# The low parts of four expert units go from VectorE to GpSimd, their high parts go ahead of the second norm's root on ScalarE

## What is computed

```python
        mix = jnp.concatenate([rec, att], axis=-1) @ w_out[l]
        x = x + g1[:, None, :] * mix
        h2 = _rms(x, norm2_g[l]) * (1.0 + sc2[:, None, :]) + sh2[:, None, :]
        x = x + g2[:, None, :] * _hier_moe(h2, w_rg[l], b_rg[l], w_re[l], b_re[l], w1[l], w3[l], w2[l])

def _hier_moe(h, w_rg, b_rg, w_re, b_re, w1, w3, w2):
    g_logits = hf @ w_rg + b_rg                     # best of 4 groups
    e_logits = (hf @ w_re + b_re).reshape(-1, 4, 4) # best 2 experts of that group
    ...
    for e in range(N_EXPERTS):                      # 16
        he = jax.nn.silu(hf @ w1[e]) * (hf @ w3[e])
        y = y + combine[:, e:e + 1] * (he @ w2[e])
```

## Time and profile before

| | us |
|---|---|
| runs before, median of 3 (lowest, highest) | 1921.34 (1917.24, 1923.22) |
| profiled execution, whole | 1922.14 |
| its span, first to last instruction | 1920.5 |
| TensorE busy | 1845.2 |
| VectorE busy | 1441.2 |
| ScalarE busy | 990.5 |
| GpSimd busy | 163.8 |

### The profile page before, as it was taken

How to read it: one execution, slowest core, us unless ns; L and a number is a source line. 1 busy time by engine, 2 the same in 40 slices (tenths; PEclk the granted TensorE clock), 3 DMA queues, 4 the chain that set the end, 5 groups by cost and what they waited for, 6 DMA issues and landing times.

```text
span 1920.5 us, 28821 instructions
## 1 busy us (share of the span) xinstructions
PE 1845.2 (96%) x11109; PEld 1627.7 (85%) x11109; DVE 1441.2 (75%) x1550; ACT 990.5 (52%) x953; POOL 163.8 (9%) x149
## 2 busy tenths in 40 slices
PE   7999999999999999999999999998998589999999
PEld 6888899998888788889999888877996478888886
DVE  7555786857877765577785787786687698888888
ACT  4444566534444444446563444443344357777774
POOL 1000000000000000000000000001000134323401
PEclk9999999999999999999999999998997799999999
DMA  6555455554877455544556377755340289999995
GB/s 245 197 191 183 154 202 189 203 198 150 287 253 268 164 186 197 190 163 173 193 181 241 132 271 255 253 185 174 122 135 20 75 316 368 348 366 348 365 352 197
DMA packets 61698, 417.33 MB, mean 217 GB/s; under 512 B 7344, under 2 KB 7712, under 8 KB 13728
## 3 DMA queue, kind: packets, MB, share of 16 engines
q1 hardware_dynamic: 51392, 369.19, 53.8%
q0 software_dynamic: 10192, 46.75, 7.3%
q10 hardware_dynamic: 16, 0.01, 0.0%
HBM read 405.94 MB, written 9.98 MB: 217 GB/s over the span
## 4 chain that ended last, share of the span: by engine, by line
PE 82%; DVE 10%; DVEq 3%; issue 2%; ACT 2%; ACTq 1%; DMA 0%; POOL 0%; POOLq 0%
PE ps L1751 14%; PE ps L1750 7%; PE ps L1735 7%; PE ps L1737 7%; PE ps L1736 7%; PE ps L1852 4%; PE ps L1853 4%; PE ps L1856 4%; PE ps L840 4%; PE ps L841 4%; PE ps L842 4%; PE ps L1748 2%; DVE wlo L2185 2%; PE ps L869 2%; PE ps L871 2%
## 5 line engine op out<-in xcount | busy, mean ns | idle before, releaser
L2185 DVE TENSOR_TENSOR wlo<-raw,whi 128x2048 fp32r<-128x2048 f32 x236 | 538.2, 2289 | 194.3 <-ACT whi L2017 191.6
L2017 ACT ACTIVATE whi<-raw 128x2048 fp32r<-128x2048 f32 x236 | 450.9, 1911 | 271.6 <-PE ps L1737 113.9
L1751 PE MATMUL ps<-xT,whi 128*128 128x512 f32 x1232 | 440.3, 397 | 0.0
L1750 PE MATMUL ps<-xT,wlo 128*128 128x256 f32 x1232 | 344.5, 280 | 0.1
L1751 PEld LDWEIGHTS ps<-xT,whi 128*128 128x128 f32 x1232 | 231.8, 188 | 47.7
L1735 PE MATMUL ps<-xT,whi 128*128 128x256 f32 x928 | 264.0, 285 | 2.0 <-DVE xT L2196 2.0
L1736 PE MATMUL ps<-xT,whi 128*128 128x256 f32 x928 | 263.8, 284 | 0.0
L1737 PE MATMUL ps<-xT,wlo 128*128 128x256 f32 x928 | 263.7, 284 | 0.0
L1750 PEld LDWEIGHTS ps<-xT,wlo 128*128 128x128 f32 x1232 | 233.0, 189 | 8.9 <-DVE xT L2204 1.0
L1438 DVE TENSOR_TENSOR wlo<-raw,whi 128x2048 fp32r<-128x2048 f32 x76 | 175.0, 2304 | 20.2 <-ACT whi L1060 19.4
L2041 ACT ACTIVATE rest<-ps 128x512 f32<-128x512 f32 x88 | 52.5, 597 | 250.7 <-PE ps L1751 250.7
(11 more groups left out here) (478 smaller groups left out, 3408.9 us busy)
## 6 DMA issues: line engine op xcount, KB each, us to landing
raw<-stream SPq DMA_DIRECT2D x236, 1024.0 KB, 4.9
raw<-experts SPq DMA_DIRECT2D x76, 1024.0 KB, 7.3
mod<-experts SPq DMA_DIRECT2D x38, 1024.0 KB, 6.8
adaraw<-ada POOLq DMA_DIRECT2D x24, 1024.0 KB, 5.2
yd<-lnrow POOLq DMA_DIRECT2D x17, 512.0 KB, 8.2
lnrow<-ln_g POOLq DMA_DIRECT2D x6, 512.0 KB, 5.0
lnrow<-ln_b POOLq DMA_DIRECT2D x6, 512.0 KB, 6.2
x_sb<-x SPq DMA_DIRECT2D x1, 1024.0 KB, 5.2
```

The costliest lines, as they stand in the source:

```text
L1750: nc.tensor.matmul(bank(b, T), wl, xThi[:, k, :], start=False, stop=False)
L1751: return nc.tensor.matmul(bank(b), wh, both, start=False, stop=k == KD - 1)
L2017: act_fn(whi[:, slot, :], raw[:, slot, :], ACT.Copy).then_inc(hi_done, 1)
L2185: v.tensor_tensor(wlo[:, slot, :], raw[:, slot, :], whi[:, slot, :].bitcast(F32), ALU.subtract).then_inc(lo_done, 1)
```

## The change

GpSimd gets an `expert_lo` of its own and runs it for units 0 to 3, behind the two DMAs of L592 and behind a wait for the stream's last low part. VectorE loses these four subtractions, and gets a wait that all four low parts are there. ScalarE makes the high parts of units 0 to 2 ahead of `rms_root("2")`, and that of unit 3 behind `split_xT`. The fifth and sixth buffer for raw numbers change places, and with them the wait of the load that fills the one in `mod`.

```diff
-        raws = [raw[:, 0, :], raw[:, 1, :], raw[:, 2, :], mod[:, 0:UNIT], mod[:, UNIT:2 * UNIT], raw5[:, :]]
+        raws = [raw[:, 0, :], raw[:, 1, :], raw[:, 2, :], mod[:, 0:UNIT], raw5[:, :], mod[:, UNIT:2 * UNIT]]
...
-                elif p == 4:
+                elif p == 5:
                     sp.wait_ge(x_done, 4 * N_H2 + 4)
...
+            def expert_lo(p):
+
+                if p < RING:
+                    pool.wait_ge(used, UNITS - (UNITS - 1 - p) % RING)
+                pool.wait_ge(*expert_hi_done(p))
+                g.tensor_tensor(splits[p % SPLITS][1], raws[p % RAWS], splits[p % SPLITS][0].bitcast(F32),
+                                ALU.subtract).then_inc(lo_done, 1)
...
+            pool.wait_ge(lo_done, RING + UNITS)
+            for p in range(SPLITS):
+                expert_lo(p)
             pool.wait_ge(ev["zero_row"], 32)
...
-            rms_root("2")
-            split_xT(N_H2)
...
-            expert_hi(0)
+            for p in range(RING):
+                expert_hi(p)
+            rms_root("2")
+            split_xT(N_H2)
+            expert_hi(RING)
...
-            for p in range(1, SPLITS):
-                expert_hi(p)
...
-            expert_lo(0)
             for pair in range(4):
                 select(0, pair)
                 if pair == 0:
                     first_one_hot(1)
-            for p in range(1, SPLITS):
-                expert_lo(p)
+
+            unit_split(dve, SPLITS - 1)
```

## The result

The changed kernel takes 1930.78 us (median of 9 runs, 1927.06 to 1934.54). The kernel before takes 1922.93 us beside it (9 runs, 1916.71 to 1924.34). The ratio is 1.0044, with a 95% interval of 1.0033 to 1.0056. The forecast was 1930.5 us, slower: 9.2 us on a kernel before of 1921.34, where 7.85 us on 1922.93 was measured. The profiled execution took 1930.89 us, with a span of 1929.2 us, 8.7 us more than before.

The account below looks back on a forecast made before the run. TensorE bounds the experts, and the chain through the second norm sets when they begin. Three holds of VectorE, together +9.76 us, less 0.6 for the first copy, give +9.2 on 1921.34: 1930.5 us, range 1920 to 1935.

Parts of the forecast that it names:

- What bounds the kernel: Experts are TensorE's once the first product begins at 1547.19; the second norm is on the path, each us added counts.
- ScalarE's part: Three high parts of 1.90 us each ahead of the second norm's root, where ScalarE idles 15.16 us, cost nothing.
- The first copy: VectorE's first subtraction leaves the chain before the copy of gathered tokens: gain 0.6 us, bounds 0 and 2.19.
- GpSimd's price: One GpSimd subtraction of 2048 columns takes 4.70 us, doubled from a row of 1024 columns; upper bound 6.0.
- Its start: GpSimd's first subtraction starts at 1505.87, when its queue is no longer occupied.
- What the rows of before showed of the meeting: At 1552.74 GpSimd's 256-column operation and VectorE's small one each waited for the other, taking 1.75 and 0.63 us.
- The handover: In the second norm, GpSimd's and VectorE's two-operand operations exclude each other, the waiting one first: 2.23, 2.91, 4.62, together 9.76 us.
- the bounds of the forecast: If GpSimd goes on at once, three in a row, L1417 is late by 11.6 us: 1932.3; with 6.0 us each, 1935.
- Low part 3: Its 4.70 us end at 1526.9, 0.5 before the routing's next two-operand operation, L1464 at 1527.42: costs nothing.
- Pieces: Ports shared in short pieces: some 10 VectorE operations lose 0.19 us each, 2 us at most: 1922.7; chance 0.17.
- hidden: VectorE's small operations pass GpSimd's subtractions; only the first-copy gain of 0.6 to 2.19 is left: 1920.7 to 1919.2; chance 0.11.
- one meeting: GpSimd's subtractions slide behind the norm, one at most in the way: +2.2 to +4.7, less 0.6, 1923 to 1925.4; chance 0.06.

Follow-up runs that it names:

- experiment 1: Changed kernel with the four low parts back on VectorE, ScalarE's new order and the buffers kept: 1919.86 us, ratio to the kernel before 0.9996.
- experiment 7: The changed kernel, unchanged, run again for its distribution and a second trace: 1929.53 us, ratio to the kernel before 1.0034.
- Experiment 3: Changed kernel, but GpSimd clears the four low parts (a write with no read) instead of subtracting: 1922.11 us, ratio to the kernel before 1.0001.
- Experiment 2: Changed kernel with a pipeline drain behind each of GpSimd's four subtractions: 1929.20 us, ratio to the kernel before 1.0045.
- experiment 5: Changed kernel with only the first low part on GpSimd, the other three back on VectorE behind the copies: 1920.09 us, ratio to the kernel before 0.9994.
- experiment 9: Changed kernel with 16 zero matmuls on TensorE, eight ahead of the second half's attention transposes and one behind each head's: 1930.23 us.
- experiment 11: Changed kernel with zero matmuls at the attention transposes, GpSimd copying the raw units instead of subtracting: 1921.42 us, ratio to the kernel before 1.0000.
- experiment 10: Kernel before with zero matmuls at the attention transposes, plus 40 ahead of the tokens' turning, 60 and 40 in the routing's waits: 1919.58 us, ratio 0.9993.

## Why the prediction was right, and where it was not

**What bounds the kernel: right.** The time is that of the first product plus 373.3 to 373.4 us, and the second norm is on the path to it.

**ScalarE's part at nothing: right** (experiment 1). The other edits at nothing: no wait of TensorE in the experts has come in.

**The first copy, 0.6 us: too much.** It starts 2.11 us after the gather (1550.07 on VectorE) instead of 2.39 (1541.59 - 1539.20), so 0.28 is gained. The last eight gather products then took 1.44 us instead of 1.20, and the first product stands 7.97 us behind the gather's start, where it stood 7.99: in this execution nothing of the gain arrives. In experiment 7, the same kernel, those eight took 1.21 us and the distance is 7.74 (1553.77 - 1546.03), so there 0.25 arrives, still less than half of what the forecast had.

**GpSimd's price, 4.70: near.** 4.49 to 4.55 us. The Trainium skill's 4497 ns (GPSIMD Engine Reference, Elementwise — side-by-side cycle accounting) is what the trace shows, and the doubled row of 1024 columns was 0.2 too high. **Its start, 1505.87:** it was 1504.16, as its two small DMAs were through 1.7 us sooner. What sets that was not tried.

**What the rows of before showed of the meeting: read too widely.** The operation that lasted 0.63 us beside GpSimd is a TENSOR_SCALAR with one operand, not an operation with two inputs like those that the rule quoted by the forecast is about, so it did not bear that rule out. Experiment 3 shows that this kind is held even by a GpSimd instruction that only writes. For two operands on both sides the rows of before had the other direction alone, GpSimd's 1.75 us instead of 0.75. The part on the chip above says that engines meet at semaphores alone. These holds set that right: they are waits of VectorE on GpSimd with no semaphore between the two.

**The handover: the step of the sum that failed.** The forecast let "the one that has waited" go first, so that three operations of VectorE were held by one subtraction each: 2.23 + 2.91 + 4.62 = 9.76 us. In the changed kernel one operation was held across all three, 13.42 us, which is the case that the bounds of the forecast named: GpSimd goes on at once each time. They priced it at 11.6 us with a start 1.7 us later. Experiment 2 shows the forecast's pattern, once there are gaps. The rule as the forecast quoted it, that whichever starts first holds the ports, does not fit the trace either: the sum is recorded 0.16 us ahead of GpSimd, and lost. A recorded start may lie ahead of the moment at which ports are asked for; no run shows that moment.

**Why the total came out all the same.** Partly by luck, twice. The forecast of 1930.5 us stands on a median of three runs, 1921.34; beside the changed kernel the kernel before took 1922.93, so that 7.85 us were measured where 9.2 were forecast, and the totals differ by 0.28 us only. And within the profiled executions two errors met. The hold was 3.66 us more than forecast. Against it the second half's sum was asked for at 1504.00 instead of 1508.34, 4.34 sooner, since this execution had the better clock in the attention and the profile of before had not. 13.42 - 4.34 = 9.08 us, by which the root is later; 8.74 is left at the first product, as the router's wait was 0.32 shorter. Experiment 7 shows the other side: its mixer was late, with the second half's sum asked for at 1511.79, but GpSimd's start, 1503.57, had hardly moved, and less of GpSimd's work lay ahead of the sum. The changed kernel gives up to GpSimd what the clock gives.

**Low part 3 at nothing: right in the changed kernel, not always.** It ends at 1535.95, and the routing's first operation of that kind (L1476) starts at 1536.18, 0.23 later, where the forecast had 0.5 to spare. In experiment 7 that was held by 1.2 us.

**The rivals.** Pieces (1922.7), hidden (1920.7) and one meeting (1923 to 1925.4) fall with 1930.78 us and the holds. One meeting alone costs what the forecast took for one: experiment 5 had 2.7 us, in the 2.2 to 4.7 of that rival.

## What to carry over

Before work of two operands moves to an idle GpSimd, look at what VectorE runs at that time with both operands in on-chip memory, down to operations on two columns, and count the whole run of GpSimd's instructions as what it can cost, not one of them (up to 13.42 us for three here). If GpSimd must run there, put it beside work that was not held in these runs: operations with an operand in PSUM, and the statistics (BATCH_NORM_STATS2, 1.29 us beside GpSimd as alone). Gaps between its instructions left 10.3 us of holds (experiment 2); a single instruction held VectorE for 2.7 us (experiment 5). And where runs of a kernel fall into groups, compare the early rows of the two profiles first: here 4.4 us of clock (the first half's gate at 1503.26 before, 1498.91 changed) lay ahead of the edit and would have been taken for its effect.

## What the runs showed that was not expected

- Between two GpSimd subtractions back to back VectorE was not let in at four boundaries (changed kernel, experiment 9) and was let in at one (experiment 7), and at one between copies (experiment 11). Between the second and third MEMSET of experiment 3 its TENSOR_SCALAR, recorded at 1507.49, was not let in: the third began at 1507.71, and it ended with that. With a gap of 0.23 to 0.81 us it was let in each time. What decides without a gap is open.
- A TENSOR_SCALAR on two columns was held 1.9 us by GpSimd's MEMSET, while two-operand operations beside it were not (experiment 3).
- During the transposes of 128 columns the granted clock fell to 0.50 in every trace without fills, but in some it was back early in the products and in others it stayed down through them, so that they took 6.92 instead of 4.01 us. 16 matmuls on zeros brought the kernel before from 1922 to 1915.67 us. What decides when the clock falls was not tried.
- The router's stretch varies in the same way: at a granted clock of 1.00 VectorE's wait for the logits was 3.78 to 3.83 us, at 0.50 it was 5.20 to 5.68. It was not tried by itself.
- With TensorE busy for 5.00 of 5 us, the granted clock was 0.50 (experiment 10), behind 5 us at 0.93 in which it was busy as long.
